# Two reorderings in a chunked gated recurrence: when VectorE multiplies the last level's operands, and when ScalarE makes exp(b)

## The reference, cut to what matters

```python
q = silu(q_raw); f = lb + (1 - lb) * sigmoid(f_raw)
log_f = log(f); k = 1 - f; v = i_raw
bc = cumsum(to_chunks(log_f), axis=3)
...
def step(S, inp):
    qi, ki, vi, bi = inp
    o_inter = einsum('bhtk,bhkv->bhtv', qi * exp(bi), S)
    decay = exp(where(causal, bi[t] - bi[s], -inf))
    attn = einsum('bhtk,bhsk,bhtsk->bhts', qi, ki, decay)
    o_intra = einsum('bhts,bhsv->bhtv', attn, vi)
    b_last = bi[:, :, -1:, :]
    S_new = exp(b_last)[..., None] * S + einsum('bhsk,bhsv->bhkv', ki * exp(b_last - bi), vi)
    return S_new, o_inter + o_intra
```

## Time and profile before

| | us |
|---|---|
| median of 3 runs | 3816.53 (3816.52 to 3818.11) |
| the profiled execution | 3818.15 |
| its span in the profile | 3816.8 |
| TensorE busy | 3702.0 (97%) |
| VectorE busy | 1701.3 (45%) |
| ScalarE busy | 1177.3 (31%) |
| GpSimd busy | 1095.4 (29%) |

### The profile page before, as it was taken

The page is one execution under the profiler, slowest core; times in us unless marked ns, Lnnn a source line. Parts: engine busy times, 40 slices in busy tenths (PEclk is TensorE's granted clock), DMA queues, the critical chain, the costliest instruction groups (busy, mean ns, idle before and its releaser), DMA issues.

```text
span 3816.8 us, 42159 instructions
## 1 busy us (share of the span) xinstructions
PE 3702.0 (97%) x17644; PEld 3027.0 (79%) x17644; DVE 1701.3 (45%) x2132; ACT 1177.3 (31%) x1523; POOL 1095.4 (29%) x747
## 2 busy tenths in 40 slices
PE   6999999999999999999999999999999999999998
PEld 6888887888878876777788888887777878888886
DVE  5655624999652473224442222225657652222226
ACT  4554532222241243444321211114323241111113
POOL 3334321222233451111442222224212442222223
PEclk9999999999999999999999999999999999999999
DMA  2000011111232240001221111113111321111112
GB/s 102 28 29 28 28 62 60 56 56 53 69 133 92 97 151 34 33 33 34 100 73 49 45 50 45 50 45 120 49 33 34 105 71 46 50 44 45 50 45 77
DMA packets 64988, 229.29 MB, mean 60 GB/s; under 512 B 7200, under 2 KB 7328, under 8 KB 64672
## 3 DMA queue, kind: packets, MB, share of 16 engines
q1 hardware_dynamic: 64800, 226.60, 18.0%
HBM read 201.40 MB, written 25.17 MB: 59 GB/s over the span
## 4 chain that ended last, share of the span: by engine, by line
PE 88%; DVE 7%; issue 2%; ACT 2%; POOL 1%; DMA 1%; SPq 0%; DVEq 0%; ACTq 0%
PE psum L505 76%; PE psum L617 2%; PE psum L853 2%; PE psum L868 2%; PE psum L883 1%; DVE Ab L2130 1%; PE psum L588 0%; DVE qb L2176 0%; PE psum L702 0%; PE psum L739 0%; POOL wl L3115 0%; PE psum L641 0%; PE psum L640 0%; DVE fb L2095 0%; DVE fb L2087 0%
## 5 line engine op out<-in xcount | busy, mean ns | idle before, releaser
L3115 POOL TENSOR_TENSOR wl<-raw,wh 128x512 fp32r<-128x512 f32 x636 | 889.7, 1419 | 2380.1 <-ACT wh L1185 2380.1
L505 PE MATMUL psum<-hh,wh 128*128 128x512 f32 (+2 forms) x3760 | 1188.4, 392 | 38.2 <-POOL wl L3115 15.7
L505 PE MATMUL psum<-hh,wl 128*128 128x512 f32 (+2 forms) x3760 | 1149.8, 381 | 0.0
L505 PE MATMUL psum<-hl,wh 128*128 128x512 f32 (+2 forms) x3760 | 1145.3, 380 | 0.0
L505 PEld LDWEIGHTS psum<-hh,wh 128*128 128x128 f32 x3760 | 678.4, 191 | 185.6 <-issue 31.2
L505 PEld LDWEIGHTS psum<-hh,wl 128*128 128x128 f32 x3760 | 699.5, 190 | 134.4
L505 PEld LDWEIGHTS psum<-hl,wh 128*128 128x128 f32 x3760 | 698.1, 189 | 133.1
L1185 ACT ACTIVATE wh<-raw 128x1024 fp32r<-128x1024 f32 x318 | 335.0, 1054 | 790.9 <-PE psum L505 784.8
L505 PE MATMUL psum<-hdh,wh 128*128 128x512 f32 x1024 | 334.0, 398 | 5.0 <-DVE B L3016 4.4
L505 PE MATMUL psum<-hdh,wl 128*128 128x512 f32 x1024 | 331.3, 395 | 0.0
L505 PE MATMUL psum<-hdl,wh 128*128 128x512 f32 x1024 | 331.3, 396 | 0.0
(11 more groups left out here) (421 smaller groups left out, 3020.3 us busy)
## 6 DMA issues: line engine op xcount, KB each, us to landing
raw<-in_wts SPq DMA_DIRECT2D x318, 512.0 KB, 3.5
keep_x<-B SPq DMA_DIRECT2D x14, 512.0 KB, 5.8
X<-in_xin SPq DMA_DIRECT2D x8, 520.0 KB, 5.6
keep_sz<-tmp SPq DMA_DIRECT2D x8, 512.0 KB, 2.9
av<-keep_gr SPq DMA_DIRECT2D x8, 512.0 KB, 3.3
tmp<-keep_sz SPq DMA_DIRECT2D x8, 512.0 KB, 3.6
av<-keep_gc SPq DMA_DIRECT2D x8, 512.0 KB, 3.9
xc<-keep_x SPq DMA_DIRECT2D x8, 512.0 KB, 5.8
```

The source lines that it names most:

```text
L505: ins = pe.matmul(out, w, x[:, k, c0:c0 + width], start=first and n == 0, stop=final and n == 2)
L3115: gp.tensor_tensor(wl[:, s, a], raw[:, s, a], fp(wh[:, s, a]), SUB).then_inc(*c.lo.tick(i, p))
```

## The change

On VectorE the multiplication of the last level's left operand (line 2175) moves up to stand between the differences of the next head's decay (`hgrn_decay`) and the decay product (`hgrn_kd`), with its wait for the last level's exponentials written out. The qe product and the right operand's product follow the decay product at once, and taking out level four (`keep(4)`) comes behind them. On ScalarE exp(b), with its wait for level three's products, moves ahead of the next head's decay. The number of `yield`s stays the same on both engines, so nothing moves against the projections.

```diff
@@ scalar, hgrn(h)
             if ahead:
                 hgrn_log(ahead)
             yield from pause(2)
+            se.wait_ge(*c.hg_pe("A", h, 3, 1))
+            se.activation(lev(LAST + 2), bx, EXP).then_inc(*c.hg_act.tick("qe", h))
             if ahead:
                 hgrn_decay(ahead)
-            yield
-            se.wait_ge(*c.hg_pe("A", h, 3, 1))
-            se.activation(lev(LAST + 2), bx, EXP).then_inc(*c.hg_act.tick("qe", h))
-            yield from pause(5)
+            yield from pause(6)
             if ahead:
                 hgrn_exps(ahead, 0)
             yield from pause(2)
@@ vector, hgrn(h)
             keep(3)
             if ahead:
                 hgrn_decay(ahead)
+            ve.wait_ge(*c.hg_act("e", h, LAST))
+            ve.tensor_tensor(kx, kx, lev(LAST + 1), MUL)
             yield from pause(2)
             if ahead:
                 hgrn_kd(ahead)
-            yield
-            keep(4)
             ve.wait_ge(*c.hg_act("qe", h))
             ve.tensor_tensor(qe, qe, q, MUL).then_inc(*c.hg_dve.tick("qe", h))
-            yield
             ve.wait_ge(*c.hg_dve("qe", h))
-            ve.tensor_tensor(kx, kx, lev(LAST + 1), MUL)
             ve.tensor_tensor(q, q, lev(LAST), MUL).then_inc(*c.hg_dve.tick("right", h, LAST))
-            yield from pause(2)
+            yield
+            keep(4)
+            yield from pause(3)
             keep(LAST)
             yield from pause(3)
             if ahead:
```

More of the change, by code:

```diff
@@ L2168, in hgrn @@
                 hgrn_kd(ahead)
+            ve.wait_ge(*c.hg_act("qe", h))
+            ve.tensor_tensor(qe, qe, q, MUL).then_inc(*c.hg_dve.tick("qe", h))
+            ve.wait_ge(*c.hg_dve("qe", h))
+            ve.tensor_tensor(q, q, lev(LAST), MUL).then_inc(*c.hg_dve.tick("right", h, LAST))
             yield
             keep(4)
-            ve.wait_ge(*c.hg_act("qe", h))
-            ve.tensor_tensor(qe, qe, q, MUL).then_inc(*c.hg_dve.tick("qe", h))
-            yield
-            ve.wait_ge(*c.hg_dve("qe", h))
-            ve.tensor_tensor(kx, kx, lev(LAST + 1), MUL)
-            ve.tensor_tensor(q, q, lev(LAST), MUL).then_inc(*c.hg_dve.tick("right", h, LAST))
-            yield from pause(2)
+            yield from pause(3)
             keep(LAST)
```

## The result

| | before, us | after, us |
|---|---|---|
| median of 4 runs each | 3816.53 (3815.54 to 3818.11) | 3795.86 (3795.24 to 3796.67) |
| the profiled execution | 3818.15 | 3796.67 |
| its span | 3816.8 | 3795.4 |

The ratio is 0.9946, with a 95% interval of 0.9933 to 0.9958: faster by 20.7 us. The forecast was 3795.5. Lines have moved by one or two: L2175 of before is L2166 now, L2172 is L2171, L2176 is L2173, L2130 is L2129, L2107 is L2106, L3115 is L3114 and L1344 is L1343.

The account below looks back on a forecast made before the run. TensorE, 97% busy, was held to bound the kernel, stalling at the last level for VectorE's right operand. Savings of 16.8 + 3.8 + 0.4 = 21.0 us gave 3795.5 against the median 3816.53; range 3788 to 3805.

Parts of the forecast that it names:

- The price of a stall: Last level on TensorE, head one: 2.99 lost waiting plus 1.31 and 0.42 of slow work, 4.72 us.
- The sum: All eight heads: 16.8 for heads one to six, 3.8 head zero, 0.4 head seven, 21.0 us saved.
- The left operand moved into idle time: VectorE, L2175 ahead of the decay product: cost nothing, covered by 1.14 idle; L2107 moves by 0.05 at most.
- Level four last: VectorE, L2130 behind the right operand's product: saves nothing, since GpSimd's difference holds L2172 back until 173.29 anyway.
- The bank's margin: Bank of the last level's second half, freed by the first L2130: in time, with 0.13 to spare.
- exp(b) ahead of the decay: ScalarE: cost nothing; Silu then waits for TensorE, and GpSimd's L3115 asks about 0.26 earlier, at 173.21.
- The collision: GpSimd's L3115 asks 0.12 before VectorE's L2176, which ends at 175.59; TensorE idles 1.66 instead of 2.83.
- The clock: TensorE behind the last level's restart: granted clock stays at 1.00 after 1.66 idle, as after 1.56 elsewhere.
- the rival of the falling clock: Clock still falls after 1.66 idle: 1.73 more lost per head, 3805.9 in all six, 3800.7 in three; chance 0.22.
- VectorE wins the ports in every head: Rival: L2176 goes ahead of GpSimd's L3115, 3.84 saved a head, 27.2 in all, 3789.3 us; chance 0.20.
- a moved wait: Rival: the bank freed by L2130, or ScalarE behind level three, eats the gain; within 0.2% of 3816.5; chance 0.05.
- the late decay product: Rival: decay product pushed behind GpSimd's difference, right operand 1.1 later in seven heads, 3824.4 us; chance 0.03.

Follow-up runs that it names:

- VectorE's half: The full change with ScalarE's part as before: exp(b) stays behind the decay, VectorE's reordering kept; 3789.45 us, ratio 0.9931.
- the run with GpSimd's difference late: The full change, with GpSimd's difference for the next head's level zero moved behind the weight difference; 3781.42 us, ratio 0.9911, the fastest.
- the late difference alone: The kernel before, with only GpSimd's difference for the next head's level zero moved behind the weight difference; 3810.29 us, ratio 0.9985.
- ScalarE's half alone: The kernel before, with only exp(b) moved ahead of the decay on ScalarE, VectorE as before; 3827.4 us, ratio 1.0026.

## Why the prediction was right

**The price of a stall.** The 4.72 for head one (2.99 waiting, 1.73 slow clock) stands. From the start of one last level to the start of the next, heads one to six, the kernel before takes 58.12, the full change 55.31, VectorE's half 54.29, and the run with GpSimd's difference late, in which the last level waits for nothing, 53.42. So a stall cost 4.70 before (forecast 4.72), 1.89 after (1.92), and 0.87 with VectorE first (0.88). The 0.10 that the prediction put down for restarting had no row behind it; the level after a restart takes 1.80 where an undisturbed one takes 1.71. With no stall left the time fell by 34.6 us against the same chip's 3816.01, where 33 was worked out; with the waiting left and only the slow clock removed, it fell by 11.4, where 12 was. Who reads only the list of waits would have priced the whole at 19.5.

**The sum.** From the point at which TensorE is ready for head zero's last level (115.94 before, 115.06 after) to the start of head seven's (521.58 and 499.76) the profiles show 405.64 and 384.70: 20.9 less, forecast 21.0. That the median came within 0.4 of the forecast is closer than the measurement can vouch for, since the interval of the ratio is some 10 us wide; the agreement head by head is the better test.

**The left operand moved into idle time.** Free, as said: the decay product starts 1.32 behind L2101, 0.03 more than before. Alone it gives the whole gain (3789.29).

**Level four last.** Nothing, as said (1.0001). The bank's margin held as well: no wait on L2129 appears.

**exp(b) ahead of the decay.** I gave it no gain, and one side effect: Silu comes to wait for TensorE, and the weight difference asks 0.26 earlier. The row shows a wait of 0.68 for TensorE and GpSimd ahead by 0.13, where I had 0.12. Alone it makes the kernel slower (1.0026).

**The collision.** L2176's successor reads 2.23 long, forecast 2.26; TensorE's idle time is 1.64, forecast 1.66; head zero's is 0.40, forecast 0.55 less the 0.16 of overlap. The waits add up to 10.2, forecast 10.5; head seven has none left, and the 0.4 saved there came as about 0.3. That GpSimd would be first rested on a margin of 0.12, taken from a modelled end; it held in heads one to six, by 0.11 to 0.13, but a margin of that size was the least safe part of the order of events, as its rival's chance of 0.20 said.

**The clock.** The weakest step was that an idle time of 1.66 would leave it full, argued from one row with 1.56. It did, in all heads. The trace of before had better rows for it, one ahead of the heads and one behind them:

```profile
22.88 0.60 PE L564 MATMUL psum<-cst,rr 16*128 16x16 f32 x2 [1.70 <-DVE rr L2040]
...
596.32 2.80 PE L702 MATMUL psum<-tmp,cst 128*8 128x512 f32 x4 [2.25 <-ACT tmp L1380]
```

After the 1.70 the granted clock stays at 1.00 for the next 3 us, after the 2.25 it falls to 0.50. So an idle time as long as the one forecast was there to be read, and the rival of the falling clock, priced at 0.22, could have been held to be less likely; the nearest fall stood at 2.25 and not at 2.83. How near 1.66 was to a limit the runs don't say: in all ten traces idle times of up to 1.78 (the longest at 39.14 of the late difference alone) kept 1.00, 2.12 was followed by a fall, and from 2.25 up it went either way.

**The rivals.** "VectorE wins the ports in every head" was priced at 3789.3, and two kernels in which it does win them gave 3789.45 and 3789.29. The rivals of the falling clock (1.00 behind the restart in every head), of a moved wait and of the late decay product have nothing in the trace for them. Of the expectations, two missed: ScalarE's half alone (3827.4 against at most 3824), and the late difference alone (3810.3 against 3813 or 3801), and in both the waits came as expected and the fall of the clock did not.

## What to carry to other kernels

Price a stall of TensorE by the distance from when it could have started to when it is back in step, not by the idle time in the list: here 4.7 for 2.8. When two engines share ports, a reordering of one is worth what it changes in who asks first: a shorter queue on VectorE gained nothing where GpSimd held the ports (level four last), an earlier exponential on ScalarE lost time through a third engine's request that came 0.26 earlier, and moving one GpSimd instruction off that place gained some 14 us on top of the change (3795.86 to 3781.42), but only 5.7 in the kernel before, where the left operand still stood in the queue. Of this change only one move earns anything, so test the parts apart before keeping them together.

## What the runs showed of the hardware that was not expected

Idle times of one length end in different clocks. With 2.33 of idle time before the last level, head four kept 1.00 and head five fell to 0.54 over the next 3 us (above). The same shows at a wait outside the recurrence that no edit touched, in rows of the kernel after and of the late difference alone:

```profile
1411.86 1.93 PE L823 MATMUL psum<-sgw,vg 128*64 128x128 f32 x16 [2.71 <-DVE vg L2454]
```

```profile
1424.40 1.09 PE L823 MATMUL psum<-sgw,vg 128*64 128x128 f32 x16 [2.71 <-DVE vg L2455]
```

The same products after the same idle time take 1.93, at a granted clock of about 0.5, or 1.09, at 1.00. At another such wait, the four products of L702 take 2.80 after 2.25 of idle time in the kernel before, 2.39 after 2.28 in the kernel after, and 1.88 after 2.26 in the fastest kernel. So a stretch far from an edit can take about a microsecond more in one kernel than in another. That the edit shifts the moment at which the stall falls would explain it; whether it is the moment alone that decides was not tried. Before the last level, no fall was seen at 1.64 in six heads, at 2.82 it fell in all six, and at 3.83 it lasted nearly twice as long in some heads as in others. Elsewhere, ahead of the product at 3772.85 of the kernel before, TensorE idled 2.77 and the clock stayed at 1.00: the length of an idle time does not settle it.

Between GpSimd and VectorE the ports were handed over in turns of one instruction, and the one that had waited went next: with both engines having a second instruction ready, neither kept the ports for two (in the kernel before: left operand's product, first half of the weight difference, right operand's product, second half). The Trainium skill (SBUF — State Buffer, Who interferes with whom) has the first to issue hold them for its whole instruction and the other blocked. The rows agree (1.22 alone, 2.23 to 2.30 behind half a weight difference of 1.29); margins of 0.09 to 0.15 in the time of asking went with the order in every head that was read, in both directions.
